# A decoder trunk on one core: 26 projection chunks per layer as one 512-column product against rounded weights, their two halves added by GpSimd

## What is computed

```python
for l in range(DEPTH):                      # DEPTH = 2
    x = layer_norm(ALPHA * x + 0.5 * swiglu(x, wg, wu, wd))
    z = x @ w_in[l]                         # 1024 -> 6400 columns
    z_s5, z_lx, z_ly, z_rw, z_gate = split(z)
    y_s5, y_lru, y_rw = s5(z_s5), rglru(z_lx, z_ly), rwkv7(z_rw)
    gates = sigmoid(z_gate)                 # 3 x 1024 columns
    merged = gates[0] * y_s5 + gates[1] * y_lru + gates[2] * y_rw
    x = layer_norm(ALPHA * x + merged @ mix_w_out[l])
    k, v = split(mem @ wkv[l])              # 256 memory tokens
    x = layer_norm(ALPHA * x + attention(x @ wq, k, v) @ wo)
    x = layer_norm(ALPHA * x + 0.5 * swiglu(x, ...))
```

## Time and profile before

| | us |
|---|---|
| median of 3 runs | 1608.58 |
| lowest and highest | 1608.37, 1609.64 |
| span of the profiled execution (first to last instruction) | 1606.9 |
| median less that span | 1.7 |
| TensorE busy, share of the span | 1578.1, 98% |
| VectorE busy | 1248.4, 78% |
| ScalarE busy | 795.6, 50% |
| GpSimd busy | 223.1, 14% |

### The profile page before, as it was taken

One profiled execution on the slowest core, in us unless ns is written; L12 is line 12 of the kernel. 1 busy time (PEld: TensorE's weight loads), 2 busy tenths in 40 slices (PEclk: granted clock), 3 DMA queues, 4 the chain that ended last, 5 costly groups with the idle time before them and its releaser, 6 DMA issues. The chain is left out here.

```text
span 1606.9 us, 31358 instructions
## 1 busy us (share of the span) xinstructions
PE 1578.1 (98%) x13277; PEld 1419.2 (88%) x13277; DVE 1248.4 (78%) x1624; ACT 795.6 (50%) x1018; POOL 223.1 (14%) x163
## 2 busy tenths in 40 slices
PE   9999999999999999999999999999999999999997
PEld 8888899999999988888888888999999999888886
DVE  6799789798667858766688998898976778587666
ACT  4655453763454545444455555346533545454443
POOL 2024500000000302001110435000000003010101
PEclk9999999999999999999999999999999999999999
DMA  8766654433536545666676665554345465456663
GB/s 250 215 191 183 183 142 139 134 116 113 178 114 205 177 133 164 192 186 193 207 197 187 190 180 153 159 157 123 106 139 151 128 208 164 143 165 190 189 191 131
DMA packets 380915, 267.74 MB, mean 167 GB/s; under 512 B 21132, under 2 KB 361576, under 8 KB 380776
## 3 DMA queue, kind: packets, MB, share of 16 engines
q1 hardware_dynamic: 377548, 255.16, 53.5%
q10 hardware_dynamic: 3228, 10.58, 2.0%
HBM read 264.66 MB, written 1.05 MB: 165 GB/s over the span
## 5 line engine op out<-in xcount | busy, mean ns | idle before, releaser
L1829 DVE TENSOR_TENSOR ring_lo<-ring_raw,ring_hi 128x1024 fp32r<-128x1024 f32 x461 | 591.9, 1288 | 193.7 <-ACT ring_hi L1410 189.3
L1410 ACT ACTIVATE ring_hi<-ring_raw 128x1024 fp32r<-128x1024 f32 x472 | 497.6, 1057 | 455.3 <-PE bank L765 204.2
L762 PE MATMUL bank<-xT,ring_hi 128*128 128x512 f32 x1344 | 335.5, 391 | 0.0
L762 PEld LDWEIGHTS bank<-xT,ring_hi 128*128 128x128 f32 x1344 | 244.2, 189 | 45.5
L735 PE MATMUL bank<-xT,ring_hi 128*128 128x256 f32 x864 | 252.2, 292 | 4.0 <-DVE region_a L2293 3.6
L736 PE MATMUL bank<-xT,ring_hi 128*128 128x256 f32 x864 | 245.1, 284 | 0.0
L737 PE MATMUL bank<-xT,ring_lo 128*128 128x256 f32 x864 | 244.9, 283 | 0.0
L765 PEld LDWEIGHTS bank<-xT,ring_lo 128*128 128x128 f32 x1344 | 183.3, 190 | 13.3 <-DVE ring_lo L1829 0.3
L765 PE MATMUL bank<-xT,ring_lo 128*128 128x256 f32 x1344 | 187.5, 282 | 0.0
L735 PEld LDWEIGHTS bank<-xT,ring_hi 128*128 128x128 f32 x864 | 166.1, 192 | 10.0 <-DVE region_a L2293 3.9
L736 PEld LDWEIGHTS bank<-xT,ring_hi 128*128 128x128 f32 x864 | 166.2, 192 | 0.6 <-issue 0.5
(11 more groups left out here) (353 smaller groups left out, 2514.7 us busy)
## 6 DMA issues: line engine op xcount, KB each, us to landing
ring_raw<-in_w_in_dram SPq DMA_DIRECT2D x100, 512.0 KB, 4.0
ring_raw<-in_ffn_wg_dram SPq DMA_DIRECT2D x88, 512.0 KB, 4.1
ring_raw<-in_ffn_wu_dram SPq DMA_DIRECT2D x88, 512.0 KB, 4.0
ring_raw<-in_ffn_wd_dram SPq DMA_DIRECT2D x88, 512.0 KB, 3.6
ring_raw<-in_xa_wkv_dram SPq DMA_DIRECT2D x32, 512.0 KB, 3.9
ring_raw<-in_s_glu_w_dram SPq DMA_DIRECT2D x16, 512.0 KB, 3.4
ring_raw<-in_mix_w_out_dram SPq DMA_DIRECT2D x16, 512.0 KB, 4.3
ring_raw<-in_xa_wq_dram SPq DMA_DIRECT2D x16, 512.0 KB, 4.3
```

Source lines behind the costliest of these rows:

```text
L762: mm(both, hi[:, k, :], xT_both[:, :, k, :], start=(k == 0), stop=(k == ND - 1), skip_group_check=True)
L1410: return nc.scalar.activation(o, i, func, **kw)
L1829: st.mark(tt(lo_flat(n), raw_flat(n), hi_flat(i), ALU.subtract), s_lo["dve"])
```

## The change

For 26 chunks of a layer (z1 to z12, every gate but gate4, k1 to k3) `half_chunk` now takes the wide form. Such a chunk claims a bank for each of its pieces, so two per chunk, and `ROTA` is longer. ScalarE copies each piece's bank of 512 columns to SBUF as it is (`half_copy`, into one of four places: parts of `work` for z, the S5 matrices `s_b` and `s_c`, no longer needed, for gates and keys), which frees the bank. GpSimd adds the two halves of the place (`half_sum`, 256 columns) into the tile where the chunk belonged before. ScalarE waits for the sum four pieces back before it overwrites a place. The gates' sigmoid is then an instruction of its own in SBUF (`gate_sigmoid`), the GELU of z4 and z5 one instruction of 1024 columns after the S5 one. Semaphores that told of read-out chunks are replaced by those of the sums.

```diff
+def added_later(kind, j):
+    return kind == "z" and j != 0 or kind == "gate" and j != 4 or kind == "k" and j != 0
+def banks_of(kind, j):
+    return 2 if added_later(kind, j) else BANKS_OF.get(kind, 0)
+SUMS = [x for x in PLAN if added_later(*x)]
...
-ROTA = [(x, b) for x in PLAN for b in range(BANKS_OF.get(x[0], 0))]
+ROTA = [(x, b) for x in PLAN for b in range(banks_of(*x))]
...
-        memT = [rounded("memT_hi", r_at, 0, ND, M), rounded("memT_lo", r_at, 2048, ND, M)]
+        memT_both = rounded("memT", r_at, 0, 2, ND, M)
+        memT = [memT_both[:, i, :, :] for i in range(2)]
...
+        halves_z = [view(work, 4096 + 512 * i, 2, T) for i in range(4)]
+        halves = [view(r, 512 * i, 2, T) for r in (bT, cT) for i in range(2)]
...
+        def half_count(kind, j, m):
+            return 2 * SUMS.index((kind, j)) + m + 1
+        def half_place(kind, j, m):
+            return (halves_z if kind == "z" else halves)[(half_count(kind, j, m) - 1) % 4]
         def released(item, b):
             kind, j = item
+            if added_later(kind, j):
+                return s_half, half_count(kind, j, b)
...
-                elif kind in WIDE:
+                elif kind in WIDE or added_later(kind, j):
                     n, o = number(kind, j, m), claim(kind, j, m)
                     pe.wait_ge(s_hi, SPLIT_AT[n] + 1)
                     hi = slot(ring_hi, SPLIT_AT[n] % SPLIT, ND, P)
                     both = o[:, :].rearrange("p (a t) -> p a t", a=2)
                     for k in range(ND):
-                        mm(both, hi[:, k, :], xT_both[:, :, k, :], start=(k == 0), stop=(k == ND - 1), skip_group_check=True)
+                        mm(both, hi[:, k, :], (memT_both if kind == "k" else xT_both)[:, :, k, :], start=(k == 0), stop=(k == ND - 1), skip_group_check=True)
                     lo = take(kind, j, m)[1]
...
-                            pe.wait_ge(*at(s_z, 2))
+                            pe.wait_ge(*at(s_hsum, half_count("z", ZORD[1], 1)))
...
+                def half_copy(kind, j, m):
+                    n = half_count(kind, j, m)
+                    if n > 4:
+                        act.wait_ge(*at(s_hsum, n - 4))
+                    act.wait_ge(*at(s_piece, INDEX[(kind, j, m)] + 1))
+                    st.mark(f(half_place(kind, j, m), bank(rota(kind, j, m), 2, T), ACT.Copy), s_half)
...
-                    done_chunk(act, "z", j)
-                    func = ACT.Gelu_apprx_tanh if j in (4, 5) else ACT.Copy
-                    st.mark(f(dst[j], bank(rota("z", j), 2, T), func), s_z)
+                    if j == ZORD[0]:
+                        done_chunk(act, "z", j)
+                        st.mark(f(zu[:, 0:2, :], bank(rota("z", j), 2, T), ACT.Copy), s_z)
+                    else:
+                        half_copy("z", j, 0)
+                        half_copy("z", j, 1)
...
+                    if g:
+                        act.wait_ge(*at(s_hsum, half_count("z", ZORD[-1], 1)))
...
+                def gate_sigmoid(j):
+                    act.wait_ge(*at(s_hsum, half_count("gate", j, 1)))
+                    g = gates[:, 2 * (j % 4):2 * (j % 4) + 2, :]
+                    st.mark(f(g, g, ACT.Sigmoid), s_gact)
                 hi_to("gate", 1, 0)
-                gate_evac(0)
+                act.wait_ge(*at(s_y5, NW))
+                half_copy("gate", 0, 0)
+                half_copy("gate", 0, 1)
...
+                half_copy("gate", 1, 0)
+                half_copy("gate", 1, 1)
                 for t in range(NW):
                     act.wait_ge(*at(s_y5d, t + 1))
                     st.mark(f(zu[:, t, :], zu[:, t, :], ACT.Gelu_apprx_tanh), s_ys5)
-                gate_evac(1)
-                gate_evac(2)
+                st.mark(f(ly, ly, ACT.Gelu_apprx_tanh), s_lyg)
+                half_copy("gate", 2, 0)
+                half_copy("gate", 2, 1)
+                gate_sigmoid(0)
+                gate_sigmoid(1)
                 act.wait_ge(*at(s_ys5, NW))
                 act.wait_ge(*at(s_ops, 1))
                 st.mark(f(zu_r[0], zu, ACT.Copy), s_zuh)
-                gate_evac(3)
+                half_copy("gate", 3, 0)
+                half_copy("gate", 3, 1)
...
+                gate_sigmoid(2)
+                gate_sigmoid(3)
...
+                    if i < 3:
+                        half_copy("gate", 5 + i, 0)
...
-                        gate_evac(5 + i)
+                        half_copy("gate", 5 + i, 1)
+                    if i >= 1:
+                        gate_sigmoid(4 + i)
 
                 for c in range(NC):
                     hi_to("gate", 8 + c)
+                    half_copy("gate", 8 + c, 0)
...
-                    gate_evac(8 + c)
+                    if c >= 1:
+                        gate_sigmoid(7 + c)
+                    half_copy("gate", 8 + c, 1)
...
-                    k_evac(j)
+                    half_copy("k", j, 0)
+                    half_copy("k", j, 1)
...
+                dve.wait_ge(*at(s_lyg, 1))
...
+                def half_sum(o, kind, j, m):
+                    pool.wait_ge(*at(s_half, half_count(kind, j, m)))
+                    x = half_place(kind, j, m)
+                    st.mark(tt(o, x[:, 0, :], x[:, 1, :], ALU.add), s_hsum)
+                z_to = {1: zu[:, 2:4, :], 2: lx[:, 0:2, 3:], 3: lx[:, 2:4, 3:], 4: ly[:, 0:2, :], 5: ly[:, 2:4, :]}
+                z_to.update({6 + k: zrw[:, 2 * k:2 * k + 2, 1:] for k in range(7)})
+                for j in ZORD[1:]:
+                    for m in range(2):
+                        half_sum(z_to[j][:, m, :], "z", j, m)
+                def gate_sum(j):
+                    if j >= 4:
+                        pool.wait_ge(*at(s_m, j - 3))
+                    for m in range(2):
+                        half_sum(gates[:, 2 * (j % 4) + m, :], "gate", j, m)
+                gate_sum(0)
                 pool.wait_ge(*at(s_nrm, 1))
                 st.then(tt(kkn, kkn, NEG_HALF.to_broadcast([P, 2 * NT * NW]), ALU.pow), s_nrr)
+                for j in (1, 2, 3, 5, 6, 7, 8, 9, 10, 11):
+                    gate_sum(j)
+                for j in range(1, 4):
+                    for m in range(2):
+                        half_sum(kmT[:, 2 * j + m, :], "k", j, m)
```

More of the change, by code:

```diff
@@ L532, in released @@
             if kind == "z":
-                return s_z, ZORD.index(j) + 1
+                return s_z, 1
             if kind == "gate":
@@ L1556, in _ @@
                 prep_evac("bT", (2, 3))
-                dst = {0: zu[:, 0:2, :], 1: zu[:, 2:4, :], 2: lx[:, 0:2, 3:], 3: lx[:, 2:4, 3:],
-                       4: ly[:, 0:2, :], 5: ly[:, 2:4, :]}
-                dst.update({6 + k: zrw[:, 2 * k:2 * k + 2, 1:] for k in range(7)})
                 act.wait_ge(*at(s_bce, 6))
```

19 lines of the change are left out of this document (12 added, 7 removed).

## The result

| | median us | runs from .. to | ratio to before, 95% interval |
|---|---|---|---|
| kernel before | 1608.47 | 1606.87 to 1609.64 | 1 |
| changed kernel | 1636.66 | 1634.92 to 1639.12 | 1.0175 [1.0161, 1.0188] |

The change costs 28.2 us. The forecast was slower, but 1613.4 us and at most 1620: it had the direction and one sixth of the size. The profiled execution took 1636.64 us with a span of 1634.8.

What follows compares the result with a forecast made beforehand. The prediction took TensorE (busy 98%) as the bound, with VectorE nearly as full in z. Product gains against additions and closer banks came to +2.4 us a layer, +4.8 in two: 1608.6 + 4.8 = 1613.4 us, range 1602 to 1620.

Steps and rivals of the forecast that it cites:

- Step 1: Wide product on TensorE: 0.09 us gained a piece, 104 pieces, 9.4 us if nothing else changes.
- Step 2: ScalarE's additional copies and sigmoids, 22 us a layer, hidden in its free time; costed at nothing.
- Step 3: GpSimd's additions delay VectorE: 0.33 us a hit, seven tenths hitting, 0.24 us an addition on average.
- Step 4: Two banks a chunk tie TensorE to VectorE's S5 reads in z: 2.5 us late at the end of z5.
- Step 5: From z5 to the end of gate3: 2.3 us late at the transposes, L1086.
- Step 6: Rest of the layer: later gates gain 0.5 and 0.7, gate9b costs 0.5, v0 0.8; sum 0.1 us.
- (D): Rival: VectorE is blocked for the whole 0.63 us of an addition; layer about +9.5, total 1627.6 us; 5%.
- (C): Rival: every addition hits VectorE, at 0.42 us; layer +5.8, total 1620.2 us; 15%.
- (B): Rival: closer banks bind, additions cost VectorE nothing; layer −2.9, total 1602.8 us; 22%.

Runs made afterwards that it cites:

- e1: Changed kernel with GpSimd's additions cut from 256 columns to 8, the rest of the change kept: 1604.87 us.
- e4: Changed kernel with three pieces a layer (in z11, gate 3 and k3) multiplied twice, right ahead of TensorE's three longest waits: 1626.27 us.
- e3: Changed kernel with S5's skip addition, the read of S5's output bank, moved about 3.9 us forward in VectorE's order: 1626.42 us.
- e10: Kernel before with 24 idle GpSimd copies of 256 columns a layer in the z stage: 1609.45 us.
- e2: Kernel before with 24 GpSimd additions of 256 columns a layer in the z stage, on data nobody uses: 1620.39 us.
- e9: Kernel before with the change in z alone, all gates and keys as before: 1621.29 us.
- e5: Changed kernel without its z part, so only gates 0 to 3, 5 to 11 and keys 1 to 3 changed: 1620.74 us.
- e8: Changed kernel with S5's skip addition moved forward and gate 3's and k3's second pieces multiplied twice: 1623.03 us.
- e7: Kernel before with 12 idle GpSimd additions of 512 columns a layer in the z stage: 1620.51 us.
- e6: Kernel before with the change for gates 5 to 11 alone; z, gates 0 to 3 and keys as before: 1606.87 us.

## Why the prediction was wrong, step by step

**Step 1** was right in its own terms. Two wide pieces of the changed kernel start at 494.04 and 496.84, 2.80 us apart where 2.79 was forecast. Even without the additions (e1) only some 3 us of its 9.4 arrive. That fits VectorE as the bound in z, the bank waits of e1 (1.5 us a layer) and v0, which the keys reach early there too (a wait of 1.2 us a layer).

**Step 2** was right that ScalarE's work is hidden: it took on 35.0 us (44 were forecast for two layers), and no wait of TensorE for a copy of a changed chunk stands in the list of waits.

**Step 3 failed, in size.** It took 0.33 us a hit and seven tenths of additions hitting, 0.24 us each. The share was about right, 16 of 21 in z, but a hit is 0.5 to 0.55 us, which makes 0.39 in z, close to the upper bound. The two values of the earlier trace rows, 0.42 and 0.29, were met beside multiplications whose second operand is a small table of columns or of constants (L2610, L2615). I took both for the price of an addition of two full operands, which takes 0.73 us alone and not 0.63. The trace of the kernel before had one of that form, between the rows that I read:

```profile
112.19 0.73 POOL L2612 TENSOR_TENSOR work<-work 128x256 f32<-128x256 f32 x1
```

I also looked for hits in the wrong place. The forecast "L1829 with a mean of 1.35 us or more in z" is wrong; the subtraction was not touched in z, and the hits lie on its neighbours (L2237 and L2238 had 685 ns each before, L2230 had 404):

```profile
L1894 DVE TENSOR_TENSOR ring_lo<-ring_raw,ring_hi 128x1024 fp32r<-128x1024 f32 x21 | 25.7, 1222 | 0.4
L2230 DVE TENSOR_TENSOR_SCAN work<-small,work 128x128 f32<-128x128 f32 x32 | 13.5, 482 | 0.3
L2237 DVE TENSOR_TENSOR work<-work,region_r 128x512 f32<-128x512 f32 x8 | 7.7, 957 | 0.0
L2238 DVE TENSOR_TENSOR work<-work,region_r 128x512 f32<-128x512 f32 x8 | 6.0, 749 | 0.0
```

Of the 16 hits in z, nine fall on two lines (L2237, L2230): the additions come a fixed time after each piece and meet the same instructions again and again. An average over VectorE's mix was the wrong model. Nor are only instructions with two operands in SBUF hit, as the step assumed: two TENSOR_SCALAR of 256 columns with one (L2283, at 292.69 and 293.43) took 0.82 us each instead of 0.35. Those that read PSUM kept their lengths (L2221: 682 ns, 688 before).

**Step 4** named the right waits and the right releaser. Sizes: z11b 3.9 us late (257.41 against 253.48) for a forecast of 2.5, z2b 7.2 (275.72 against 268.55) for 3.1. Its statement that the S5 products behind z11b come "about when VectorE is ready" is where it broke: they came 3.16 us after that. Those 3.16 us (0.46 before) are 2.7 of the 4.1 us that z2b is later than forecast.

**Step 5 failed, in its path.** It forecast 2.3 us late at the transposes, with a wait of 0.8; it was 9.5, with a wait of 2.97. The same VectorE instructions in both traces, start in us, make a ledger:

| VectorE instruction | before | after | late | what came in between |
|---|---|---|---|---|
| first S5 read (L2180, now L2245) | 253.19 | 256.87 | 3.7 | 8 hits, 4.2; 0.2 us of waiting gone; 0.2 early at 216 us |
| next S5 product read (L2156, L2221) | 259.93 | 266.31 | 6.4 | its wait for TensorE 3.16 instead of 0.46 |
| second S5 read | 268.25 | 275.19 | 6.9 | 1 hit, 0.5 |
| last S5 read | 296.66 | 305.82 | 9.2 | 8 hits, 3.9; two waits, 1.6, gone |
| RWKV's scans (L2231, L2296) | 299.86 | 306.33 | 6.5 | a wait of 2.7 for ScalarE gone |
| bonus product ahead of the transposes (L2277, L2342) | 325.84 | 335.36 | 9.5 | 6 hits, 3.0 |

The step had the scans follow ScalarE's sigmoids, 1.4 us late. In the changed kernel they follow VectorE's own last read with no wait:

```profile
305.82 0.48 DVE L2245 SCALAR_TENSOR_TENSOR region_z<-region_z,param_columns,bank 128x256 f32<-128x256 f32 x1
306.33 2.44 DVE L2296 TENSOR_TENSOR_SCAN region_r<-constants,work 128x256 f32<-128x256 f32 x4
```

So the 8 hits between the second and the last S5 read, for which the prediction charged nothing (it only let TensorE gain 0.6 us there), were on the path; so were six hits behind the scans instead of three, and 2.7 us more of waiting. On a chain that VectorE binds there is no gain of TensorE to credit.

**Step 6** had gate9b at 0.5 us, measured 0.50. It had v0 pushed by 0.8 us; TensorE waits 2.73 us there, since the wide keys bring it to v0 sooner while VectorE comes later.

**Missing altogether:** what a long wait does to the clock. In the kernel before TensorE's waits in z, at the transposes and at v0 are under 0.3 us, and no row shows a price behind a wait. The prediction put it at nothing without saying so. e4 takes back 10.4 us of the error of 23 (between the profiled executions 10.9: 8.9 behind the transposes, 2.0 ahead of them). What is left is steps 3 to 5, hits and waits of VectorE, and all of it hangs on the additions, as e1 shows; the repairs overlap (e3 alone gains 10.2 us, both together 13.6), so that no split of the 23 us into independent parts is shown.

Among the rivals, (D) had a layer at +9.5 us, the figure that the first transposes show, but by luck: D charged additions only up to z2b, at 0.63 each, and had 2.0 us of keys in it. It got 5% because rows 7 spoke against "blocked for the whole 0.63 us"; the measured hit of 0.54 lies nearer to D's 0.63 than to the forecast's 0.33. (C), with 0.42 an addition, had nearly the measured average of 0.39 and still came to 1620.2 us: the right price on the same path would have left 16 us unexplained. (B) described e1: 1602.8 forecast for additions that cost nothing, 1604.87 measured.

## What to carry to other kernels

Before moving elementwise work to GpSimd "because it is idle", look at which engine is nearly full in that stretch: if it is VectorE, a GpSimd instruction with two SBUF operands cost it here some 0.54 us per 256 columns when it met a VectorE instruction with two SBUF operands (or one of the TENSOR_SCALAR above), and 16 of 21 in z did. Then ask how long TensorE will wait in one go. Here single waits of 2.7 us and more amid work were followed by some microseconds at 1.2 GHz and waits up to 1.7 us were not, so that the same delay cost less in many short waits than in a few long ones. And a delay can bounce: a late TensorE makes VectorE late, so an engine's idle time in the old trace is no reserve until it is checked who ends it.

## What the runs showed of the hardware that was not expected

A full hit of GpSimd on VectorE grows with what the GpSimd instruction moves, and is shorter than that instruction: 0.54 us for an addition of 256 columns, 1.09 for 512, 0.20 for a copy of 256, where they take 0.73, 1.27 and 0.40 us alone. Where the addition has a start on VectorE's instruction, the hit is smaller: 0.42 us with a start of 0.25 (L1894 at 447.92), 0.23 with one of 0.35 (L2481 at 452.14). A GpSimd copy is thus nearly harmless where an addition isn't (e10 against e2: 1609.45 and 1620.39 us).

The price of a wait jumps with its length. All single waits of TensorE of over 1 us in the 13 traces, and how many of them had the granted clock at its lower level (1.2 GHz) in or just behind them:

| wait, us | where | waits | clock fell |
|---|---|---|---|
| 3.4 | z11b (changed kernel, e9) | 4 | 4 |
| 3.0 | transposes (changed kernel, e3, e5) | 5 | 5 |
| 2.7 | v0 (changed kernel, e3, e5) | 6 | 6 |
| 2.1 | RWKV's normalisation, for GpSimd's power (e3, e8) | 4 | 2 |
| 1.8 | gate 5, all kernels | 26 | 12 |
| 1.0 to 1.75 | low parts, banks, power, transposes | 21 | 0 |
| 2.7 to 3.4 | the first DMA, 3 us into each kernel | 13 | 0 |

A fall costs 1.7 or 3.4 us of TensorE's time. The wait ahead of gate 5 is the same 1.8 us everywhere, yet the clock fell after it in one of the two layers (the second of the kernel before, below, and the first of the changed kernel, 388 to 396), in both (e2, e9) or in neither (e5, e7, e8). That it costs the kernel before and the changed kernel the same 1.7 us is therefore luck; what decides it stays open. It also colours the tables by layer: of e6's 0.5 and −1.4 us behind the transposes, +1.7 and −1.7 are this stretch, which e6 has in the first layer and the kernel before in the second, and 1.7 of e9's 2.6 us are the same. The waits at the start don't follow the rest either: hardly any work of TensorE lies ahead of them (5 matmuls in the first 4 us of the kernel before).

```profile
1172.00:1180.00 8.00, 6.18 (x135) 5.98 (x132) 5.44 (x9) 0.90 (x2) 0.00 (x0) 0.79 0.27 78
```
